# A chunked recurrence in a two-layer decoder trunk: square roots taken for four chunks at once, and the last four chunks normalised beside the out-projection

## The reference, cut to what matters

```python
def step(state, xs):                      # bt: cumulated log of the forget gate
    qt, kt, vt, bt = xs
    rel = jnp.where(tri, bt[..., :, None, :] - bt[..., None, :, :], -jnp.inf)
    att = jnp.einsum('bhtd,bhsd,bhtsd->bhts', qt, kt, jnp.exp(rel))
    o = jnp.einsum('bhts,bhsv->bhtv', att, vt) + \
        jnp.einsum('bhtd,bhdv->bhtv', qt * jnp.exp(bt), state)
    b_last = bt[:, :, -1:, :]
    new_state = jnp.exp(b_last[:, :, 0, :])[..., None] * state + \
        jnp.einsum('bhsd,bhsv->bhdv', kt * jnp.exp(b_last - bt), vt)
    return new_state, o
...
o_b = rms_norm(hgrn2(bq, bf, bi, lb), b_out_norm_g).reshape(b, s, 512)
o_b = o_b * silu(bg)
mix = jnp.concatenate([o_a, o_b], axis=-1) @ even_w_out
```

## Time and profile before

| | us |
|---|---|
| median of 3 runs (2717.45 to 2719.07) | 2718.35 |
| the profiled execution's own time | 2719.63 |
| its span, first to last instruction | 2717.9 |
| TensorE busy in the span | 2502.4 (92%) |
| VectorE, GpSimd, ScalarE busy | 1591.4, 1353.7, 1051.3 |
| mean granted TensorE clock | 0.957 of 2.4 GHz |

### The profile page before, as it was taken

One profiled execution on the slowest core, in us unless ns is written; L12 is line 12 of the kernel. 1 busy time (PEld: TensorE's weight loads), 2 busy tenths in 40 slices (PEclk: granted clock), 3 DMA queues, 4 the chain that ended last, 5 costly groups with the idle time before them and its releaser, 6 DMA issues.

```text
span 2717.9 us, 31347 instructions
## 1 busy us (share of the span) xinstructions
PE 2502.4 (92%) x11111; PEld 1989.0 (73%) x11133; DVE 1591.4 (59%) x2354; ACT 1051.3 (39%) x1741; POOL 1353.7 (50%) x770
## 2 busy tenths in 40 slices
PE   6899798789778899999999989989998999999999
PEld 4677676345677688888888877766677888888887
DVE  6478568984786554445554655656444446544472
ACT  4255587555443432223232144525443222322220
POOL 4201233887664165456665813127615566654591
PEclk9999899799899899999999999988988999999999
DMA  4211122000300211122110222102002122111211
GB/s 148 51 28 28 32 63 87 22 8 5 124 16 1 62 46 39 39 62 62 56 38 30 77 97 55 62 15 75 20 13 64 53 62 62 53 33 37 62 54 70
DMA packets 164002, 136.57 MB, mean 50 GB/s; under 512 B 22969, under 2 KB 137730, under 8 KB 163906
## 3 DMA queue, kind: packets, MB, share of 16 engines
q1 hardware_dynamic: 152658, 124.58, 15.2%
q10 hardware_dynamic: 11248, 10.75, 1.5%
HBM read 116.17 MB, written 13.63 MB: 48 GB/s over the span
## 4 chain that ended last, share of the span: by engine, by line
PE 73%; DVE 8%; issue 8%; ACT 4%; POOL 4%; DMA 0%; ACTq 0%; another core or an unknown queue 0%; DVEq 0%; POOLq 0%
PE ps L2150 22%; PE ps L2151 21%; PE ps L2152 21%; PE ps L2345 1%; ACT signs L1218 1%; POOL diag L837 1%; PE ps L2262 1%; POOL cl L892 1%; PE ps L2504 1%; DVE ub L2043 1%; PE ps L2333 1%; PE ps L2353 1%; POOL w_lo L722 1%; DVE shared L2040 1%; PE ps L2344 1%
## 5 line engine op out<-in xcount | busy, mean ns | idle before, releaser
L2150 PE MATMUL ps<-h_hi,w_hi 128*128 128x512 f32 x1680 | 673.0, 401 | 13.6 <-POOL w_lo L740 9.7
L2151 PE MATMUL ps<-h_lo,w_hi 128*128 128x512 f32 x1680 | 662.0, 394 | 0.0
L2152 PE MATMUL ps<-h_hi,w_lo 128*128 128x512 f32 x1680 | 661.5, 394 | 0.0
L2150 PEld LDWEIGHTS ps<-h_hi,w_hi 128*128 128x128 f32 x1680 | 320.4, 191 | 83.2 <-issue 14.4
L722 POOL TENSOR_TENSOR w_lo<-w_raw,w_hi 128x1024 fp32r<-128x1024 f32 x73 | 182.7, 2503 | 378.0 <-ACT w_hi L1228 375.5
L2151 PEld LDWEIGHTS ps<-h_lo,w_hi 128*128 128x128 f32 x1680 | 320.6, 191 | 68.3 <-issue 3.9
L2152 PEld LDWEIGHTS ps<-h_hi,w_lo 128*128 128x128 f32 x1680 | 319.8, 190 | 67.9
L2040 DVE TENSOR_TENSOR x_res<-ps,x_res 128x1024 f32<-128x1024 f32 x224 | 268.8, 1221 | 115.1 <-PE ps L2152 115.1
L2021 DVE TENSOR_TENSOR u_all<-ps,u_all 128x512 f32<-128x512 f32 x112 | 77.4, 691 | 416.0 <-ACT u_all L1125 416.0
L740 POOL TENSOR_TENSOR w_lo<-w_raw,w_hi 128x1024 fp32r<-128x1024 f32 x112 | 267.0, 2401 | 104.2 <-ACT w_hi L1114 104.2
L2150 PE MATMUL ps<-w_hi,uo_hi 128*128 128x512 f32 x784 | 307.6, 392 | 3.1 <-DVE shared L2040 3.1
(11 more groups left out here) (349 smaller groups left out, 4573.9 us busy)
## 6 DMA issues: line engine op xcount, KB each, us to landing
w_raw<-in_mlp_w_up SPq DMA_DIRECT2D x64, 512.0 KB, 4.1
w_raw<-in_mlp_w_down SPq DMA_DIRECT2D x64, 512.0 KB, 3.8
w_raw<-in_even_w_in SPq DMA_DIRECT2D x23, 512.0 KB, 3.7
x_res<-in_x SPq DMA_DIRECT2D x16, 512.0 KB, 8.5
w_raw<-in_odd_w_in SPq DMA_DIRECT2D x10, 512.0 KB, 3.7
scr_x<-x_res SPq DMA_DIRECT2D x8, 512.0 KB, 2.6
x_res<-scr_x SPq DMA_DIRECT2D x8, 512.0 KB, 5.0
out<-x_res SPq DMA_DIRECT2D x8, 512.0 KB, 2.6
```

The lines of the kernel that those rows point to most:

```text
L2150: t_.matmul(out_, ah, bh, start=first, stop=False)
L2151: t_.matmul(out_, ah, bl, start=False, stop=False)
L2152: return t_.matmul(out_, al, bh, start=False, stop=last)
```

## The change

- **Roots.** Sums of squares go to `o_ss` and roots to `o_sd`, both columns of `rq`. ScalarE takes the roots of chunks 0 to 3 in one instruction of 16 columns at slot 34 (chunk 4, l = 6), those of chunks 4 to 7 at slot 62.
- **Outputs.** At R_SQUARE ScalarE writes the squares into `kf` in SBUF, whose chunk is used up, and copies bank 5 to `o_sum`; bank 5 is free after that.
- **Norms of chunks 0 to 3** follow at four-slot steps: norm (DVE) and transposes (PE) at slots 36, 40, 44, 48, gate (DVE) at 39, 43, 47, 51, rounding (ACT) at 40 to 52, remainder at 41 to 53, now on GpSimd.
- **Norms of chunks 4 to 7** follow behind the last slot: the transposes of 4, 5 and 6 behind the out-projection's tile 0, into banks 7, 5 and 6, that of 7 behind tile 1; VectorE gates 4 to 6 ahead of its additions of tile 0, and 7 behind them.
- **Keys' exponents.** VectorE's difference is gone. ScalarE takes exp(-bT + last) for each head, four instructions with `last` as bias.

```diff
-        R_OUT, R_SQUARE, R_STATE, R_ROOT, R_NORM, R_TURN, R_GATE, R_HIGH, R_LOW = 1, 4, 5, 6, 7, 6, 9, 10, 11
+        R_OUT, R_SQUARE, R_STATE = 1, 4, 5
-        HG_SLOTS = 7 * T + R_LOW + 1
+        ROOTS = {7 * 4 + 6: 0, 7 * T + 6: 4}
+        N_NORM, N_TURN, N_GATE, N_HIGH, N_LOW = 36, 36, 39, 40, 41
+        LAST_BANK = {4: 7, 5: 5, 6: 6, 7: 7}
+        HG_SLOTS = 7 * T + 9
+        def normed_chunk(n, first):
+            d, rem = divmod(n - first, 4)
+            return d if rem == 0 and 0 <= d < 4 else None
...
+            def normed_low(d):
+                dk = slice(d * P, (d + 1) * P)
+                pool.wait_ge(hg["o_hi"], d + 1)
+                g.tensor_tensor(h_lo[:, 4:8, dk], chunk_values(o_den, d), h_hi[:, 4:8, dk].bitcast(F32), ALU.subtract) \
+                    .then_inc(hg["o_lo"], 1)
...
-                        act.wait_ge(hg["kl_arg"], c + 1)
-                        s.activation(ek[:], ek[:], ACT.Exp, scale=-1.0).then_inc(hg["kl_exp"], 1)
+                        for h in range(4):
+                            ins = s.activation(ek[:, h * P:(h + 1) * P], bT[:, h, tk], ACT.Exp, scale=-1.0,
+                                               bias=bT[:, h, c * P + P - 1:c * P + P])
...
-                    s.activation(ps[:, 7, :], ps[:, 5, :], ACT.Square).then_inc(hg["o_sq"], 1)
-                d = after_chunk(n, R_ROOT)
+                    act.wait_ge(hg["s_done"], d + 1)
+                    s.activation(kf[:, d, :], ps[:, 5, :], ACT.Square).then_inc(hg["o_sq"], 1)
+                    s.activation(chunk_values(o_sum, d), heads(ps[:, 5, :]), ACT.Copy).then_inc(hg["o_out"], 1)
+                if n in ROOTS:
+                    d = ROOTS[n]
+                    act.wait_ge(hg["o_ss"], d + 4)
+                    s.activation(o_sd[:, 4 * d:4 * d + 16], o_ss[:, 4 * d:4 * d + 16], ACT.Sqrt, scale=1.0 / P, bias=epsc[:]) \
...
+            def normed(d):
+                o = chunk_values(o_sum, d)
+                dve.wait_ge(hg["o_out"], d + 1)
+                v.tensor_tensor(o, o, o_sd[:, 4 * d:4 * d + 4].unsqueeze(2).to_broadcast((P, 4, P)), ALU.mult) \
...
-                    if l == L_KL_ARG:
-                        v.tensor_tensor(heads(ek[:]), bT[:, :, tk], last, ALU.subtract).then_inc(hg["kl_arg"], 1)
...
+            invert_roots(4)
+            for d in range(4, T):
+                normed(d)
+            for d in range(4, 7):
+                gated(d)
+            add_and_norm(1, G_OUT0 + 16, lambda: gated(7))
...
+                    if t == 0:
+                        for d in (4, 5, 6):
+                            turn_normed(d)
+                    if t == 1:
+                        turn_normed(7)
```

More of the change, by code:

```diff
@@ L900, in _ @@
                     split_low(U_OUT0 + 4 + c // 2 - 1)
+                d = normed_chunk(n, N_LOW)
+                if d is not None:
+                    normed_low(d)
             split_low(U_OUT0 + 7)
+            for d in range(4, T):
+                normed_low(d)
             pool.wait_ge(hg["att_read"], 8 * T)
@@ L1368, in _ @@
                 if d is not None:
-                    act.wait_ge(hg["o"], d + 1)
-                    if d:
-                        act.wait_ge(hg["o_full"], d)
-                    s.activation(ps[:, 7, :], ps[:, 5, :], ACT.Square).then_inc(hg["o_sq"], 1)
-                d = after_chunk(n, R_ROOT)
-                if d is not None:
[L1376 to L1382, removed]
+                    act.wait_ge(hg["s_done"], d + 1)
[5 more added lines that the diff above has]
+                    s.activation(o_sd[:, 4 * d:4 * d + 16], o_ss[:, 4 * d:4 * d + 16], ACT.Sqrt, scale=1.0 / P, bias=epsc[:]) \
+                        .then_inc(hg["o_sd"], 1)
+                d = normed_chunk(n, N_HIGH)
+                if d is not None:
+                    normed_high(d)
                 if l == L_SPLIT and c >= 2 and c % 2 == 0:
                     round_last(c // 2 - 1 if c < T else 3)
+            for d in range(4, T):
+                normed_high(d)
             norm(1)
@@ L1507, in add_and_norm @@
                             add_bank(g0 + 2 * t + hf, t, hf, first_bank(phase))
+                        if t == 0 and after_first is not None:
+                            after_first()
                         norm_tile(phase, t)
@@ L1999, in _ @@
                                       heads(ps[:, i % 4, :])).then_inc(hg["att_read"], 1)
-            add_and_norm(1, G_OUT0 + 16)
+            invert_roots(4)
+            for d in range(4, T):
+                normed(d)
+            for d in range(4, 7):
+                gated(d)
+            add_and_norm(1, G_OUT0 + 16, lambda: gated(7))
             def mlp_by_halves(layer):
@@ L2485, in _, with turn_normed @@
             attention(0, QS0, QL0, KS0, VH0, VL0, PH0, PL0, diag0, identb0, nearb0)
+            def turn_normed(d):
+                bank = LAST_BANK.get(d, 7)
+                pe.wait_ge(hg["o_norm"], d + 1)
+                if bank == 7:
+                    pe.wait_ge(hg["o_full"], 5 if d == 7 else d)
+                elif bank == 5:
+                    pe.wait_ge(hg["o_out"], T)
+                else:
+                    pe.wait_ge(hg["s_ready"], T)
+                for h in range(4):
+                    ins = t_.transpose(ps[:, bank, h * P:(h + 1) * P], chunk_values(o_sum, d)[:, h, :], ident[:])
+                ins.then_inc(hg["o_turned"], 1)
             for n in range(HG_SLOTS):
@@ L2538, in _ @@
                     ins.then_inc(hg["s_done"], 1)
[L2539 removed]
+                d = normed_chunk(n, N_TURN)
                 if d is not None:
[L2541 to L2545 removed]
+                    turn_normed(d)
                 if n in OA_SLOTS:
```

65 lines of the change are left out of this document (29 added, 36 removed).

## The result

The changed kernel takes 2720.51 us (median of 20 runs, 2717.86 to 2724.14), the kernel before 2716.70 in the runs beside it (20 runs, 2710.77 to 2719.91). The ratio is 1.0015 with a 95% interval of 1.0009 to 1.0021: slower by about 4 us. That is within 0.2% and within the range, but on the other side of the kernel before than the forecast.

What follows compares the result with a forecast made beforehand. A chunk was taken as a chain across engines that no engine fills, the out-projection as bound by TensorE. Terms summed to -2.45 us, which against the median 2718.35 gave 2715.9 us; range 2709.5 to 2722.5.

Steps and rivals of the forecast that it cites:

- longer stretch at half clock: Rival: chunk 2's half-clock stretch comes back in two more chunks, 1.69 us each, giving 2719.3 us; chance 0.17.
- Chunk 5: Window longer by 1.6 us: remainder 1.3, norm 0.45, transposes 0.35, less 0.5 for GpSimd being disturbed less.
- the +0.45 of the prediction: Slot 40: the norm, now with both operands in SBUF, falls beside two GpSimd multiplications, +0.45 us, bounds 0 and 1.1.
- Chunk 2: TensorE's idle 0.65 us and the transposes' 0.85 go: -1.5 us, at worst 0.7 won.
- Chunk 6: The transposes stay and only TensorE's idle time goes: -0.7 us, bounds 0 and 2.2.
- First part: Recurrence's first difference to chunk 2; chunk 1's term: transposes go and GpSimd's multiplications are disturbed less, -1.75 us.
- the clock holds: Rival: TensorE stays at 2.4 GHz with shorter pauses, ScalarE's whole gain comes through, sum -8.35, 2710.0 us; chance 0.28.
- Chunk 7: Last chunk: transposes and their wait before the block go, part comes back at half clock: -1.0 us, bounds 0.65 and 2.15.
- The out-projection: TensorE busy throughout; four groups of transposes instead of one, 3 x 0.35 = +1.05 us.
- Chunk 3's -0.5: GpSimd is disturbed less, so the product behind the weight remainder comes some 0.45 us earlier: -0.5 us.
- The rival on GpSimd: All four remainders, each with a locked-out neighbour, land on the path at slots 41, 45, 49, 53: 2722.4 us; chance 0.10.

Runs made afterwards that it cites:

- filler: Unread TensorE products put into two of its waits in chunks 2 to 7: changed kernel 2711.52 us (0.9976), kernel before 2715.33 us (0.9985).
- the eight listed above: Profiles timed from the recurrence's first difference to chunk 2: six of changed kernels alike up to there, 50.10 to 52.08 us; two of kernels before, 52.90 and 52.52.
- the one with memsets: The changed kernel with 12 small chained memsets on VectorE at slot 9: 2720.59 us, 1.0006 of the kernel before.
- the control: The changed kernel as it is, timed once more beside the kernel before on another chip: 2720.05 us, 1.0005 [0.9996, 1.0014].

## Why the prediction was wrong

**The step that failed** is one that the sum doesn't have: it left the stretches at half clock where they were. In chunk 4 a 0 for roots and loads and 0.35 for transposes stood against +3.03, in chunk 3 -0.5 against +2.18. The runs show that work is not the reason: with the clock at 1.00 in both kernels they are +0.35 and +0.02 (24.46 to 24.11, 23.49 to 23.47). The rival *longer stretch at half clock* named this, with 1.69 us for each of two chunks; it was 2.1 (5.88 - 3.74) in chunk 3, 2.7 in chunk 4 and 1.6 in chunk 5. What spoke for that rival, that clock drops came in every second half, should have weighed more than 0.17, since chunk 2 of the kernel before already showed what one costs. That the time still fell inside the range is no merit of the sum: the range was wide enough for parts of both rivals. One reading of the prediction needs care as well: the clock fell to 0.50 at 735.0 us, inside the pause of 2.97 us and 1.4 us ahead of the product at 736.39, and not behind it.

**Chunk 5**, predicted +1.6, measured +4.19. GpSimd after:

```profile
805.65 1.51 POOL L909 TENSOR_TENSOR cl<-cl,kq 128x512 f32<-128x512 f32 x1 [1.39 <-ACT cl L1375]
...
809.89 1.72 POOL L894 TENSOR_TENSOR h_lo<-o_den,h_hi 128x512 fp32r<-128x512 f32 x1
811.57 4.35 POOL L909 TENSOR_TENSOR cl<-cl,kq 128x512 f32<-128x512 f32 x3
```

From the product ahead of the weight remainder to the one wanted it takes 811.57 - 805.65 = 5.92, where it took 812.35 - 808.08 = 4.27: +1.65 where +1.3 was taken. The product at 805.65 itself comes 6.46 us behind the chunk's start, where it was 6.00: GpSimd idles 1.39 us ahead of it for ScalarE, and ScalarE for VectorE's difference at 803.68, ahead of which a norm now stands (802.03). The norm takes 1.02 us from start to start, and the difference, 1.14 instead of 1.58, gives 0.44 back. That is the +0.45 of the prediction in size, but it was reckoned as a longer norm; the size is partly luck. Remainder and norm make the last level product come 2.14 us later from the chunk's start (14.39 against 12.25). The transposes add 0.46. The rest is the clock: the block behind 813.58 ran in part at half clock, +1.57. TensorE's wait ahead of it grew to 2.83 us, but that this wait brought the half clock isn't shown. For it: with the remainder on GpSimd and filler the pause is 3.34 us and the block's first matmul takes 0.77, and with the remainder on VectorE the clock stays at 1.00; but that second kernel also has ten products instead of four at this place. Against it: with the remainder on VectorE and no filler the wait is 0.86 us, and product and block took 6.04 us, more than the 5.31 here.

**VectorE and the norms.** VectorE after, its wait for TensorE in chunk 4, two norms of chunk 5 with the difference behind the first, and the first `xn`:

```profile
791.53 0.69 DVE L1981 TENSOR_TENSOR x_res<-ps,x_res 128x512 f32<-128x512 f32 x1 [8.48 <-PE ps L2190]
...
802.03 1.10 DVE L1959 TENSOR_TENSOR o_sum<-o_sum,rq 128x512 f32<-128x512 f32 x1
...
803.68 1.14 DVE L1990 TENSOR_TENSOR cl<-bT 128x512 f32<-128x512 f32 x1
...
810.40 1.75 DVE L1959 TENSOR_TENSOR o_sum<-o_sum,rq 128x512 f32<-128x512 f32 x1
...
892.08 0.75 DVE L1509 TENSOR_SCALAR xn<-x_res,rstd 128x1024 f32<-128x1024 f32 x1
```

These two norms take 1.10 and 1.75 us, where one took 0.69 with an operand in PSUM; the other two of the early chunks, at 780.51 and 831.92 us, fall where GpSimd idles and take 0.69 and 0.68. The norm of 1.75 us overlaps GpSimd's remainder (809.89 to 811.61) and ends 0.54 us behind it. The Trainium skill ("SBUF — State Buffer", section "SBUF: two separate sides") has such a pair lock each other out for a whole instruction, and these rows agree. Right: VectorE isn't short of time, its wait for TensorE grew from 4.12 to 8.48. Right too: `xn` is there at 892.83, 892.7 was predicted, and nothing waits for it; the transposes that take it start at 894.35, 894.5 was predicted.

**ScalarE.** Timeline after: the keys' exponentials of chunk 3, then slot 34 with the roots of four chunks:

```profile
757.93 1.26 ACT L1381 ACTIVATE ek<-bT 128x128 f32<-128x128 f32 x4
...
778.59 1.28 ACT L1409 ACT_TABLE_LOAD   x1
779.88 0.31 ACT L1409 ACTIVATE rq<-rq,epsc 128x16 f32<-128x16 f32 x1
780.10 1.04 ACT L1250 ACTIVATE w_hi<-w_raw 128x1024 fp32r<-128x1024 f32 x1
781.15 1.28 ACT L1374 ACT_TABLE_LOAD   x1
```

Only two table loads stand here, and there is one more in the rest of the recurrence, as predicted. The four exponentials take 1.26, predicted 1.1. From the load's end to the rounding 0.23 us passes again, so the drain of 1380 ns that the Trainium skill gives ("ScalarE: Activation LUTs", section "What ACT_TABLE_LOAD costs") isn't seen here either.

**The gains** were real, and two of them undersized. Chunk 2: -2.84 for -1.5; its last level product comes 1.70 earlier, and the block behind it lost most of its half-clock time as well (4.28 against 5.43 us with the product). Chunk 6: -1.61 for -0.7; I had taken only TensorE's idle time, but the product behind it also comes earlier because a larger part of what precedes it runs at full clock. First part: -1.44 for -1.75 in the first profiles, and between -0.4 and -2.8 over the eight listed above, 1.6 between their means; so it was about right. In the two kernels with filler chunk 6 is -2.3, as in the rival *the clock holds* (2.2). Chunk 2 is -4.1 there, but 1.57 of it is the stretch that the kernel before keeps; without it some 2.5 are left, an estimate from 25.70 - 1.57 - 21.59, between the forecast's 1.5 and the rival's 4.5. The filler begins with chunk 2, so the first part's -2.4 there isn't at a held clock.

**Chunk 7**: -1.0 predicted, +0.13 measured. The transposes are gone and the block starts 0.76 earlier from the chunk's start (9.11 against 9.87), but more of it then runs at half clock (in the window 7.0 us instead of 3.2): "part of that comes back" was right in kind, but all of it came back. **The out-projection**: +1.38 for +1.05; a group of four transposes costs 0.46 us in TensorE's full stream, not 0.35. **Chunk 3's -0.5** was right for the keys' exponent by itself (-0.45 when put alone into the kernel before), but isn't there with the other parts: 23.49 against 23.47.

**The rival on GpSimd** fell: only the remainder at slot 41 is on the path; chunk 6, which has one as well, became shorter.

**What stays open** is what sets the length and the place of a stretch at half clock. Two causes were tried: less activity of TensorE (transposes moved away), and where the pattern of chunks falls in time. With transposes put back, the time at half clock in chunks 3 and 4 was shorter in some profiles and not gone. It was shorter, 3.4 us in each, in two kernels without added work on TensorE as well, the one with memsets and the one with the keys' exponent on VectorE, so activity can't be the whole cause. But each is a single execution, no median of these is shown to be below the changed kernel's, and the same instructions run with different patterns: chunk 4 took 27.12 and 27.10 us in the changed kernel and 24.45 in the one that differs only from chunk 5 on. A rival is left that no run settles: that the long stretches in chunks 3 and 4 are one of several patterns that either kernel can run with. The kernel before was profiled only once without filler. That half-clock time is the loss is shown by the filler; which part of the change brings it, if one does, isn't shown.

## What to carry to other kernels

When several engines pass work around and TensorE waits for some 3 us in each round, price a change by what it does to the waits as well as by the work it moves: read the clock column window by window, ask which instructions will stand behind each wait, and profile a kernel more than once before a single chunk's time is believed. Don't put moved work, however short, between two products of which TensorE awaits the second; here it cost 1.65 us and made the pause 2 us longer. Where a stage of TensorE's pauses can't be closed, products that nobody reads are a cheap trial: they gave the kernel before 0.15%. The change alone lost 0.15%, or 0.05% by the control; with unread products it was 0.24% ahead of the kernel before, and 0.31% once the remainders had left GpSimd and the products were fitted to the waits. About half of that is the products' own.

## What the runs showed of the hardware

Unread products on TensorE made the kernel before faster by 0.15% (2715.33 us, 0.9985 [0.9976, 0.9994]), although TensorE got 1 to 1.6 us more of busy time in every full chunk (20.11 for 18.65 in chunk 4). In the rows of TensorE the time per matmul of 512 columns in a block is 0.23 us between starts at full clock and 0.43 at half. The same instructions ran at different granted clocks from one execution to the next: 0.93 and 0.86 over the recurrence's first 50 us (changed kernel and control), 0.92 and 0.77 over the first 21 of them, and 0.81 and 0.93 in chunk 4 (changed kernel, and the one with the remainders on VectorE).
